# Row norms reordered, w_up's product with both halves of x at once, weights' second halves in two steps, second input projection reordered

## The reference

```python
# first block, after the attention branches were merged
x = x + _rms_norm(merged @ w_out[l], g_post_mix[l])
h2 = _rms_norm(x, g_pre_mlp[l])
m = jnp.square(jax.nn.relu(h2 @ w_up[l])) @ w_down[l]
x = x + _rms_norm(m, g_post_mlp[l])
# second block
h = rms_norm(x, norm1_g[layer])
proj = h @ w_in[layer]                    # gated unit, attention
x = x + mix @ w_out[layer]
x = x + peer(rms_norm(x, norm2_g[layer]), w_query[layer], sub_keys[layer],
             expert_u[layer], expert_v[layer])
```

## Time and profile before

| | |
|---|---|
| median of three runs | 1298.29 us |
| profiled execution, whole | 1298.2 us |
| profiled execution, span | 1296.4 us |
| mean granted clock of TensorE | 0.998 |
| TensorE busy | 1282.8 us |
| VectorE busy | 939.1 us |
| ScalarE busy | 693.0 us |
| GpSimd busy | 33.8 us |

### The profile page before, as it was taken

The page is one execution under the profiler, slowest core; times in us unless marked ns, Lnnn a source line. Parts: engine busy times, 40 slices in busy tenths (PEclk is TensorE's granted clock), DMA queues, the critical chain, the costliest instruction groups (busy, mean ns, idle before and its releaser), DMA issues.

```text
span 1296.4 us, 22040 instructions
## 1 busy us (share of the span) xinstructions
PE 1282.8 (99%) x8615; PEld 1170.1 (90%) x8615; DVE 939.1 (72%) x1701; ACT 693.0 (53%) x1162; POOL 33.8 (3%) x27
## 2 busy tenths in 40 slices
PE   9999999999999999999999999999999999999998
PEld 8899989998878879999999999999988888888886
DVE  6776567774457866999899777777776666666776
ACT  6666457653455654444454555555555555554445
POOL 0000130000020010000000000000000000000000
PEclk9999999999999999999999999999999999999999
DMA  8544456666656436477767666656577677767763
GB/s 266 162 143 121 135 171 196 187 186 187 192 163 217 129 98 203 154 240 232 230 215 230 224 191 190 202 185 205 187 275 275 243 239 241 242 240 244 242 242 114
DMA packets 72808, 260.56 MB, mean 201 GB/s; under 512 B 8257, under 2 KB 9025, under 8 KB 72449
## 3 DMA queue, kind: packets, MB, share of 16 engines
q1 hardware_dynamic: 71232, 255.25, 60.6%
q0 software_dynamic: 1040, 3.34, 0.8%
q10 hardware_dynamic: 432, 0.56, 0.1%
HBM read 240.25 MB, written 18.87 MB: 200 GB/s over the span
## 4 chain that ended last, share of the span: by engine, by line
PE 94%; DVE 3%; ACT 2%; issue 1%; ACTq 0%; DVEq 0%
PE ps L1079 26%; PE ps L479 15%; PE ps L487 15%; PE ps L488 14%; PE ps L489 14%; PE ps L1040 2%; PE ps L533 1%; PE ps L664 1%; PE ps L520 1%; ACT whi L1116 1%; PE ps L526 1%; PE ps L514 1%; PE ps L999 1%; DVE wlo L1602 1%; ACT TH L1122 1%
## 5 line engine op out<-in xcount | busy, mean ns | idle before, releaser
L1602 DVE TENSOR_TENSOR wlo<-raw,whi 128x1024 fp32r<-128x1024 f32 (+2 forms) x410 | 497.8, 1216 | 284.1 <-ACT whi L1116 281.4
L1116 ACT ACTIVATE whi<-raw 128x1024 fp32r<-128x1024 f32 (+2 forms) x421 | 442.0, 1051 | 423.0 <-PE ps L1079 169.1
L487 PE MATMUL ps<-TH,whi 128*128 128x256 f32 x1504 | 431.8, 287 | 0.0
L488 PE MATMUL ps<-TL,whi 128*128 128x256 f32 x1504 | 425.1, 283 | 0.0
L489 PE MATMUL ps<-TH,wlo 128*128 128x256 f32 x1504 | 425.0, 283 | 0.0
L488 PEld LDWEIGHTS ps<-TL,whi 128*128 128x128 f32 x1504 | 288.2, 192 | 0.0
L487 PEld LDWEIGHTS ps<-TH,whi 128*128 128x128 f32 x1504 | 288.0, 192 | 0.0
L489 PEld LDWEIGHTS ps<-TH,wlo 128*128 128x128 f32 x1504 | 287.9, 191 | 0.0
L1079 PE MATMUL ps<-whi,TH 128*128 128x512 f32 x512 | 199.2, 389 | 0.0
L1079 PE MATMUL ps<-wlo,TH 128*128 128x512 f32 x512 | 199.2, 389 | 0.0
L1079 PE MATMUL ps<-whi,TL 128*128 128x512 f32 x512 | 199.2, 389 | 0.0
(11 more groups left out here) (327 smaller groups left out, 1394.4 us busy)
## 6 DMA issues: line engine op xcount, KB each, us to landing
raw<-in_expert_u_dram SPq DMA_DIRECT2D x128, 512.0 KB, 3.8
raw<-in_expert_v_dram SPq DMA_DIRECT2D x128, 512.0 KB, 4.3
raw<-in_w_up_dram SPq DMA_DIRECT2D x32, 512.0 KB, 3.6
raw<-in_w_down_dram SPq DMA_DIRECT2D x32, 512.0 KB, 4.2
acts<-stage SPq DMA_DIRECT2D x32, 512.0 KB, 4.2
stage<-acts SPq DMA_DIRECT2D x30, 512.0 KB, 3.7
raw<-in_w_in_dram SPq DMA_DIRECT2D x20, 512.0 KB, 4.2
raw<-in_w_gate_dram SPq DMA_DIRECT2D x16, 512.0 KB, 3.4
```

Source lines behind the costliest of these rows:

```text
L487: e.matmul(dst, whi[:, h, sl], xh[:, k, :], start=k == 0, stop=False)
L488: e.matmul(dst, whi[:, h, sl], xl[:, k, :], start=False, stop=False)
L1116: e.activation(whi[:, u % NH, 0:n], raw[:, u % NR, 0:n], ACT.Copy).then_inc(*hi(u))
L1602: e.tensor_tensor(wlo[:, u % NH, 0:n], raw[:, u % NR, 0:n], whi[:, u % NH, 0:n].bitcast(F32), ALU.subtract).then_inc(*lo(u))
```

## The change

**Feed-forward.** TH and TL become the two slices of one tensor T, so that for each k the 256 high columns lie right before the 256 low ones. A new function `wide_cols` multiplies a unit's `whi` with both at once, 512 columns into a whole bank, for all eight k, and then `wlo` with the high 256 columns into the bank's first half. The wait for `wlo` stands between the two. The bank's halves have then to be added: ACT copies the second half out, DVE adds the first to it, takes max(x, 0) times x in one instruction, ACT copies that into MH and DVE subtracts for ML. PE's wait for a bank is now for that sum. Relu of a unit is taken before the next split, and its high and low parts one unit later.

**Pairs.** The second unit of the two pairs (w_up's and w_query's) has its low half made by POOL in two instructions of 512 columns, and PE waits for the second of them only at k = 4.

**Row norms.** In `row_norm` the table load for the root comes after the splits, the second tile's squares before its root in a place of their own, and DVE's split of unit end + 2 after low parts of the second tile. For h3, high and low parts 4 to 7 of the first tile are interleaved with the second tile's norm, and the split of unit end + 3 is added inside it; in the loop over s it is left out, squares go from step 2 to 4, DVE's mean and scale come together at step 5, and the table of gelu is loaded at step 6.

**Last hand-over.** ACT takes the squares of (1, 0) after the first tile's high parts, DVE takes those of (1, 1) itself, and its low parts and the split of QUERY + 2 are reordered.

The diff, cut to its core:

```diff
-        TH = sb(ctx, "TH", [128, 8, 256], F32R)
-        TL = sb(ctx, "TL", [128, 8, 256], F32R)
+        T = sb(ctx, "T", [128, 8, 2, 256], F32R)
+        TH, TL = T[:, :, 0, :], T[:, :, 1, :]
...
+            def wide_cols(u, x, b, ks):
+                h = u % NH
+                e.wait_ge(*hi.at(u))
+                for k in ks:
+                    e.matmul(ps[b][:, :], whi[:, h, k * 128:k * 128 + 128], x[:, k, :, :], start=k == 0, stop=False)
+                whole(u)
+                for k in ks:
+                    m = e.matmul(ps[b][:, 0:256], wlo[:, h, k * 128:k * 128 + 128], x[:, k, 0, :], start=False, stop=k == 7)
+                return m
...
                 whole(u)
-                whole(u + 1)
+                e.wait_ge(*lo_half.at(u + 1))
                 for k in range(7):
+                    if k == 4:
+                        whole(u + 1)
...
             for n in range(2, 32):
-                whole(UP + n)
...
-                    e.wait_ge(*relu_a.at(f"r{n - 4}"))
-                cols(UP + n, 0, 8, TH, TL, ps[(n + 2) % 4][:, 0:256], range(8)).then_inc(*used(UP + n))
+                    e.wait_ge(*relu_d.at(f"sq{n - 4}" if n < 6 else f"sum{n - 4}"))
+                wide_cols(UP + n, T, (n + 2) % 4, range(8)).then_inc(*used(UP + n))
...
-                warm(ACT.Sqrt)
                 end = u0 + 2 * nu
                 for u in range(u0 + nu + 3, end):
                     split(u)
+                warm(ACT.Sqrt)
...
                 e.wait_ge(*half_used.at(name))
+                part(0, 1)
                 root(0)
                 split(end)
                 high_tile(to, 0, range(4), gain)
                 split(end + 1)
-                high_tile(to, 0, range(4, 8), gain)
+                if to == "h2.":
+                    high_tile(to, 0, range(4, 8), gain)
                 e.wait_ge(*used.at(end - 1))
+                part(1, 1)
+                if to == "h3.":
+                    high_tile(to, 0, (4, 5), gain)
                 root(1)
                 split(end + 2)
-                high_tile(to, 1, range(8), gain)
+                if to == "h3.":
+                    high_tile(to, 0, (6, 7), gain)
+                if to == "h3.":
+                    high_tile(to, 1, range(6), gain)
+                    split(end + 3)
+                    high_tile(to, 1, (6, 7), gain)
+                else:
+                    high_tile(to, 1, range(8), gain)
...
+            def relu_take(n):
...
+                    e.wait_ge(*relu_d.at(f"sq{n - 4}"))
+                at = 0 if n < 2 else 256
+                copy(mr[:, n % 4, :], ps[(n + 2) % 4][:, at:at + 256]).then_inc(*relu_a(f"r{n}"))
+
+            def relu_high(n):
+                e.wait_ge(*relu_d.at(f"sq{n}"))
+                copy(MH[:, n, :], mf[:, n % 4, :]).then_inc(*relu_a(f"high{n}"))
...
             last_root(0)
-            last_half(1, 0)
             split(QUERY)
             high_tile("x4.", 0, range(4), gain_x4)
             split(QUERY + 1)
             high_tile("x4.", 0, range(4, 8), gain_x4)
-            last_half(1, 1)
+            last_half(1, 0)
             last_root(1)
...
                 update(0, 1)
-                split(end)
                 low_tile(to, 0, range(4), gain)
-                split(end + 1)
-                low_tile(to, 0, range(4, 8), gain)
+                if to == "h2.":
+                    low_tile(to, 0, range(4, 8), gain)
                 gained(1, 1)
+                if to == "h3.":
+                    low_tile(to, 0, (4, 5), gain)
                 factor(1)
                 update(1, 0)
+                if to == "h3.":
+                    low_tile(to, 0, (6, 7), gain)
                 update(1, 1)
-                split(end + 2)
                 low_tile(to, 1, range(4), gain)
-                low_tile(to, 1, range(4, 8), gain)
+                if to == "h3.":
+                    split(end + 2)
+                low_tile(to, 1, range(4, 6), gain)
+                if to == "h3.":
+                    split(end + 3)
+                low_tile(to, 1, (6, 7), gain)
+                if to == "h2.":
+                    split(end + 2)
...
+                if n >= 2:
+                    e.tensor_tensor(mr[:, b, :], ps[(n + 2) % 4][:, 0:256], mr[:, b, :], ALU.add).then_inc(*relu_d(f"sum{n}"))
+                    e.wait_ge(*relu_d.at(f"sum{n}"))
+                e.scalar_tensor_tensor(out=mf[:, b, :], in0=mr[:, b, :], scalar=0.0, in1=mr[:, b, :], op0=ALU.max,
+                                       op1=ALU.mult).then_inc(*relu_d(f"sq{n}"))
...
             last_half(0, 1)
+            last_scale(0)
             e.wait_ge(*used.at(OUT2 + 5))
-            last_scale(0)
             last_half(1, 0)
-            last_mean(1)
-            low_tile("x4.", 0, range(8), gain_x4)
+            low_tile("x4.", 0, range(4), gain_x4)
             e.wait_ge(*used.at(OUT2 + 7))
             last_half(1, 1)
+            low_tile("x4.", 0, range(4, 8), gain_x4)
+            e.wait_ge(*last_d.at("11"))
+            square_sum(xn3[:, 1, cols512(1)], X[:, 1, cols512(1)], p4s[:, 3:4]).then_inc(*norm_d("x4.sq"))
+            last_mean(1)
             last_scale(1)
+            low_tile("x4.", 1, range(8), gain_x4)
             split(QUERY + 2)
-            low_tile("x4.", 1, range(8), gain_x4)
...
+            def split_halves(u):
+                e.wait_ge(*hi.at(u))
+                subtract(u, 0, 512).then_inc(*lo_half(u))
+                subtract(u, 512, 1024).then_inc(*lo_pool(u))
```

More of the change, by code:

```diff
@@ L339, in build @@
         lo_pool = signal("lo_pool", LO_POOL)
+        lo_half = signal("lo_half", (UP + 1, QUERY + 1))
         turned = signal("turned", (
@@ L428, in build @@
             "cq.ss cq.v cq.r cq rbc ck.ss ck.v ck.r ck out.v out.r rsq down.v down.r a.v a.r b.v b.r x4.v0 "
-            "x4.r0 x4.00 x4.01 x4.v1 x4.r1 x4.10 x4.11").split())
+            "x4.r0 x4.00 x4.01 x4.sq x4.v1 x4.r1 x4.10 x4.11").split())
         rows_d = signal("rows_d", (
@@ L441, in build @@
         relu_d = signal("relu_d", (
[3 rows of a table removed]
-            "low27 sq28 low28 sq29 low29 sq30 low30 sq31 low31").split())
[5 rows of a table added]
+            "sum31 sq31 low30 low31").split())
         fold_d = signal("fold_d", ["00", "10", "01", "11"])
@@ L1116, in split @@
                 e.activation(whi[:, u % NH, 0:n], raw[:, u % NR, 0:n], ACT.Copy).then_inc(*hi(u))
+            warmed = iter(range(16))
             def warm(func):
-                e.activation(warm_out, warm_in, func)
+                i = next(warmed)
+                e.activation(warm_out[:, i:i + 1], warm_in, func)
             def copy(dst, src, scale=1.0):
@@ L1324, in row_norm @@
                     split(u)
+                warm(ACT.Sqrt)
                 def root(t):
-                    part(t, 1)
                     e.wait_ge(*post_d.at(f"{name}.v"))
@@ L1403, in beside2 @@
             def beside2(s):
-                if s == 2:
+                if s == 4:
                     row_square("down", xn3, r3_st)
@@ L1407, in beside2 @@
                     row_root("down", r3_st)
+                elif s == 6:
+                    warm(ACT.Gelu_apprx_tanh)
                 elif s == 10:
@@ L1469, in scalar_program @@
             for s in range(48):
-                if s % 2 == 0 and s:
+                if s % 2 == 0 and s > 2:
                     split(IN2 + s // 2 + 2)
@@ L1482, in last_root @@
                 e.wait_ge(*norm_d.at(f"x4.v{t}"))
-                e.wait_ge(*last_a.at(f"{t}1"))
+                if t == 0:
+                    e.wait_ge(*last_a.at("01"))
+                else:
+                    e.wait_ge(*norm_d.at("x4.sq"))
                 e.activation(s4[:, t:t + 1], p4s[:, 2 + t:3 + t], ACT.Sqrt, bias=v4[:, t:t + 1],
@@ L2353, in pool_program, with subtract @@
         def pool_program(e):
+            def subtract(u, c0, c1):
+                return e.tensor_tensor(wlo[:, u % NH, c0:c1], raw[:, u % NR, c0:c1], whi[:, u % NH, c0:c1].bitcast(F32),
+                                       ALU.subtract)
             def split(u):
-                n = width(u)
                 e.wait_ge(*hi.at(u))
-                e.tensor_tensor(wlo[:, u % NH, 0:n], raw[:, u % NR, 0:n], whi[:, u % NH, 0:n].bitcast(F32),
-                                ALU.subtract).then_inc(*lo_pool(u))
+                subtract(u, 0, width(u)).then_inc(*lo_pool(u))
+            def split_halves(u):
+                e.wait_ge(*hi.at(u))
+                subtract(u, 0, 512).then_inc(*lo_half(u))
+                subtract(u, 512, 1024).then_inc(*lo_pool(u))
             e.wait_ge(*low.at("x5"))
@@ L2364, in pool_program @@
             e.dma_start(gb1[:, :], A["g_post_mix"].partition_broadcast(128)).then_inc(*d_gb1(0))
-            for u in (BR_B + 1, BR_B + 2, BR_B + 3, OUT, OUT + 1, UP, UP + 1):
+            for u in (BR_B + 1, BR_B + 2, BR_B + 3, OUT, OUT + 1, UP):
                 split(u)
+            split_halves(UP + 1)
             e.wait_ge(*low.at("h2.71"))
```

(2 more changed lines are left out.)

40 lines of the change are left out of this document (20 added, 20 removed), and 14 rows, old and new, of tables (relu_a, relu_d).

## The result

The changed kernel takes 1290.49 us (median of five runs, 1290.12 to 1290.70) against 1298.29, a ratio of 0.9939 (95% interval 0.9923 to 0.9955). The prediction was 1290.0. Beside it the kernel before ran five times: four times 1298.24 to 1298.55 us and once 1569.04, which no trace covers and which doesn't move the median. The profiled execution took 1290.7 us, its span is 1288.9.

What follows compares the result with a forecast made beforehand. PE, busy 1282.8 of 1296.4 us, was taken to bound the kernel. Gains of 3.2 + 1.6 + 0.6 + 2.8 = 8.2 us took 1298.2 to 1290.0 us, range 1288.0 to 1294.0.

Steps and rivals of the forecast that it cites:

- A: w_up, 30 units: 16 matmuls instead of 24, 2774 ns per unit instead of 2880, gaining 3.2 us.
- B: Passage from w_out through the row norm to w_up: three waits of PE shortened, 1.6 us in all.
- (a): End of w_out: the last unit's ACT split goes ahead of the table load and starts earlier, gaining 0.8 us.
- (c): w_out to w_up: DVE's split moves behind the second tile's low parts; 0.4 us if it works alone.
- b: w_up's first pair: POOL subtraction in halves lets four matmuls run before PE waits; 0.8 us together with (c).
- C: Passage from w_down through the row norm to w_in_2: ACT and DVE work reordered, 0.6 us, bounds 0 and 1.2.
- D: Passage from w_out_2 through the last norm to w_query: PE's 1.72 us stop goes, second tile sooner, 2.8 us gained.
- the lower bound: w_out_2 to w_query: only 1.4 us gained there if the low clock comes anyway.
- rival 1: w_up: a wide matmul takes 240 ns or DVE sets the pace, so no gain there, 1293.2 us; chance 0.09.
- rival 2: Three projection-to-norm passages: new waits replace old ones, giving 2.5 us instead of 5.0, 1292.5 us; chance 0.12.
- rival 3: w_gate, w_query, expert_u: T's new addresses slow about 3800 matmuls by 6.7 ns each, 1315 us; chance 0.05.
- its mirror: Opposite address effect: matmuls on TH and TL speed up to 113.3 ns, giving 1265 us; chance 0.03.

Runs made afterwards that it cites:

- experiment 7: Changed kernel with T behind the small constants: 1275.23 us; then T, or T and the weights, at other addresses: 1290.82, 1290.84, 1301.05 and 1295.14 us.
- experiment 4: Changed kernel with POOL's subtractions whole again: 1291.19 us; changed kernel with the second QUERY unit's subtraction cut after 384 columns instead of 512: 1290.98 us.
- experiment 6: Kernel before with only the reordering of two row norms and of the second input projection's helper work on ScalarE and VectorE: 1296.87 us.
- experiment 3: Kernel before with only the reordering of the last hand-over (w_out_2 to w_query), POOL's subtractions undivided: 1295.97 us.
- experiment 2: Kernel before with only the joined tensor T, the wide matmuls of w_up and the new relu: 1295.84 us.
- T moved: Changed kernel with T behind the small constants, 64 bytes past a multiple of 128 while the weights stay at 0: 1275.23 us.

## Why the prediction was right, and where its steps were off

**A, mechanism right, one term mis-sized.** The wide matmul was taken at 226.7 ns and is 230.0; the narrow one at 120.0 and is 118.8. A unit is 2.793 us instead of 2.774: 0.019 x 30 units = 0.57 us, the whole of the gap between 3.2 and 2.6. The step that failed is "the nearest row ... 512 columns with the same tiles in the other roles": with T moving and weights loaded the same 512 columns cost 3.3 ns more on average (230.0), though the last three of each eight do stand at 226 to 227. Why the first five don't is open. No run shows the 226.7 of the sum for T moving over a whole unit: in w_up it is 230.0 with T at 0 past, and some 233 with T 32, 64 or 96 past. Nor does a width have one price: the table of experiment 7, with 113.3 to 120.0 narrow and 226.7 to 233.3 wide, shows that it hangs on the pair of tensors. The helpers kept up with the margin that was counted.

**B, right in sum.** (a) gave 0.89 for 0.8, (c) alone 0.32 for 0.4, the halves 0.37; b and c together 0.69 for 0.8.

**C, right in sum, its terms not** (0.56 alone, 0.58 in the kernel after, for 0.6). Counted from w_down's last matmul (377.30 before, 373.33 after), PE starts on the third unit 0.71 us sooner, where 0.3 was forecast for ACT's split. But X's first update of the second tile comes no sooner than before and the second 0.53 later (0.6 was forecast); the last of the transposes that wait for them start only 0.22 sooner, so 0.49 of the gain is gone by then. The low chunks ahead of VectorE's split then give 0.34 for the forecast 0.6, and PE's next block starts 0.56 sooner. That the sum came out is in part luck. The prediction also had no term for the product that waits for POOL (experiment 4): VectorE gets there 0.51 us sooner than before and waits that out, which is why X's first update starts 3.63 us after w_down's last matmul, as against 3.62.

**The second input projection was costed at nothing and gave 0.40.** The step that failed is "beside matmuls with over 0.5 us to spare ... costed at nothing". It looked at what the moves might cost and not at what they free, and the spare time wasn't there: in the trace of before VectorE's split ends at 402.27 and PE's matmul starts at 402.32 (experiment 6).

**D, right, 2.61 for 2.8.** Transposes of the second tile were forecast at 485.3; set back by the 4.93 us that the stretches ahead gained, they came at 480.59 + 4.93 = 485.5, and the clock stayed full, as said. The 1.4 of the lower bound is 2.7 less 1.3 us for a low clock, which no run with the new order shows (1.00 here and in experiment 3); before, with 0.51 granted, matmuls of 256 columns stood 0.213 us apart instead of 0.120, 1.3 us over 14 of them. What the prediction didn't have is how the square sum and the halves hinder each other: it took the halves at half the price each, while the second one took 1.84 us instead of 1.29, behind the sum. PE's wait of 0.50 for that half stands right ahead of the transposes. The first scaled copy of the second tile, which started while it ran, took 0.79 us instead of 0.49. That this is the missing 0.2 is likely, not shown, since no run has the halves without the sum. "No wait of over 0.5 us before them" held by a hair, with 0.50 for POOL.

**Rivals.** The chances stood at 0.66 for the forecast, 0.09 for rival 1, 0.12 for rival 2, 0.05 for both together with gains given back, 0.05 for rival 3 and 0.03 for its mirror. 1 fell with experiment 2, 2 with the stretches, each being within 0.2 of its term. 3 was wrong for this change, since T's halves stayed as far past a multiple of 128 bytes as the weights' (0 for both, at bytes 65,664 and 41,088 of a partition), but right that addresses can matter: its price per matmul (6.7 ns between 113.3 and 120.0) and its mirror image, TH and TL at 113.3, are what T moved shows. The mirror's 1265 was too good by 10 us. The last stage takes 3.4 of them. The stretch of w_query and expert_u gave 19.0 where its 3,408 matmuls at 6.7 ns would give 22.7, in part since some stood at 117.8. The remaining 3 are w_gate's: its 384 matmuls would give 2.6, but they ran in part at 117.8, OAh, OBh and w_out became slower, and hand-over 1 ended no earlier than in the kernel after (201.13 against 200.79). The argument against rival 3, that slices keep a step of whole kilobytes, was the right argument for no change, and no argument that addresses don't matter.

The total was 0.5 off because 0.6 too much in A and 0.2 in D stand against 0.4 not seen in the projection. That they cancel in part is luck.

## What to carry to other kernels

Read a matmul's price from starts of neighbours, and for the same pair of loaded and moved tensors: the same shape cost up to 6% more or less with where the two lie relative to each other. If one tile's matmuls are faster than another's of the same shape, that is worth an experiment before any reordering; moving one tensor behind three small ones here gave twice what the whole change gave, and two other places for it lost 5 to 11 us. Where GpSimd and VectorE both work near the critical path, look for a wait in the duration of VectorE's instructions beside GpSimd's: the square sum took 1.69 us instead of 0.68, and even a product of one number per partition 0.77 instead of 0.16, while low chunks out of PSUM kept their 0.34. Place GpSimd's instructions so that they end when such a one of VectorE is due; here that place was worth 0.5 us.

## What the runs showed of the hardware that I had not expected

- In expert_u matmuls of 256 F32R columns stand 120.0 ns apart when loaded and moved tensor start equally far past a multiple of 128 bytes, 113.3 when T is 64 past and the weights 0 (117.8 before 535 us), 116.7 and 118.3 when T is 32 and 96 past. With 512 columns of weights moving it is 226.7 for the first, 228.9 in the last stage and 233.3 in w_out for T 64 past, and 233.3 for 32 and 96. Starts were varied in steps of 32 bytes only, and 128 isn't told from 256.
- 512 columns of T moved took 230.0 ns where 512 columns of weights took 226.7, with T and the weights both 0 past a multiple of 128.
- A VectorE square sum of 0.68 us waited out a GpSimd subtraction and ended 0.55 us after it, in three kernels; in a fourth the subtraction waited for the sum (1.84 us instead of 1.29). A VectorE product of one number per partition waited too, 0.77 us instead of 0.16.
